# Interleaving the moving columns of three-product matmuls, and placing the weight panels 64 bytes apart

## What is computed

```python
def swiglu(h, w1, w3, w2):
    return (jax.nn.silu(h @ w1) * (h @ w3)) @ w2

def moe_swiglu(h, router_w, w1, w3, w2):
    ...
    for e in range(N_EXPERTS):
        out = out + gates[..., e:e + 1] * swiglu(h, w1[e], w3[e], w2[e])
    return out

def second_block(...):
    for i in range(DEPTH):
        ...
        h_x = h_x + 0.5 * mx[2] * ffn1(pre(h_x, g_norm[i, 0], mx[0], mx[1]))
        ...
        h_x = h_x + mx[5] * ox
        h_x = h_x + 0.5 * mx[8] * ffn2(pre(h_x, g_norm[i, 2], mx[6], mx[7]))
```

## Time and profile before

| | |
|---|---|
| median of two runs | 2837.01 us (2836.5 and 2837.52) |
| the profiled execution's own time | 2839.29 us |
| its span, first to last instruction | 2837.6 us |
| PE busy | 2720.8 us, 96% of the span |
| PEld busy | 2445.7 us, 86% |
| DVE busy | 1913.8 us, 67% |
| ACT busy | 1182.6 us, 42% |
| mean traffic from HBM | 179 GB/s |
| mean granted TensorE clock | 0.989 of full speed |

### The profile page before, as it was taken

How to read it: one execution, slowest core, us unless ns; L and a number is a source line. 1 busy time by engine, 2 the same in 40 slices (tenths; PEclk the granted TensorE clock), 3 DMA queues, 4 the chain that set the end, 5 groups by cost and what they waited for, 6 DMA issues and landing times.

```text
span 2837.6 us, 43022 instructions
## 1 busy us (share of the span) xinstructions
PE 2720.8 (96%) x17542; PEld 2445.7 (86%) x17542; DVE 1913.8 (67%) x2703; ACT 1182.6 (42%) x1510; POOL 118.1 (4%) x227
## 2 busy tenths in 40 slices
PE   3979999999999999899999999999999999999999
PEld 3879998899999999888888888888888888886999
DVE  5877778765777788777477445764666646675655
ACT  3436445453443477642132424422334222255543
POOL 0010000000000000000000000000000000000000
PEclk9989999999999999999999999999999999999999
DMA  7676766635676698745355223453534534311554
GB/s 296 220 244 228 263 228 213 232 135 169 235 239 209 230 347 309 259 145 187 132 184 169 83 93 103 153 170 122 166 136 137 169 122 159 120 60 46 176 186 144
DMA packets 116619, 511.97 MB, mean 180 GB/s; under 512 B 12608, under 2 KB 16064, under 8 KB 116304
## 3 DMA queue, kind: packets, MB, share of 16 engines
q1 hardware_dynamic: 81776, 381.92, 39.5%
q0 software_dynamic: 32112, 117.45, 12.5%
q10 hardware_dynamic: 2544, 9.96, 0.9%
HBM read 508.24 MB, written 1.05 MB: 179 GB/s over the span
## 4 chain that ended last, share of the span: by engine, by line
PE 78%; DVE 11%; ACT 4%; issue 3%; DMA 2%; ACTq 0%; DVEq 0%; POOLq 0%
PE PS L2099 22%; PE PS L2101 22%; PE PS L2100 22%; DVE wlo L1102 5%; ACT whi L575 2%; PE PS L2293 1%; DMA ada_first<-in_adastream 1%; PE PS L2290 1%; PE PS L2289 1%; DVE ada L1134 1%; PE PS L2194 1%; DMA ada<-in_adastream 1%; PE PS L2195 1%; PE PS L2198 1%; DVE PS L1134 1%
## 5 line engine op out<-in xcount | busy, mean ns | idle before, releaser
L575 ACT ACTIVATE whi<-raw 128x1408 fp32r<-128x1408 f32 (+2 forms) x540 | 718.1, 1342 | 778.9 <-PE PS L2101 719.3
L1102 DVE TENSOR_TENSOR wlo<-raw,whi 128x1408 fp32r<-128x1408 f32 (+2 forms) x540 | 839.8, 1577 | 217.0 <-ACT whi L575 216.1
L2099 PE MATMUL PS<-h_hi,whi 128*128 128x256 f32 (+1 forms) x2656 | 859.2, 324 | 15.5 <-DVE wlo L1102 8.4
L2100 PE MATMUL PS<-h_lo,whi 128*128 128x256 f32 (+1 forms) x2656 | 858.7, 323 | 0.0
L2101 PE MATMUL PS<-h_hi,wlo 128*128 128x256 f32 (+1 forms) x2656 | 858.6, 323 | 0.0
L2099 PEld LDWEIGHTS PS<-h_hi,whi 128*128 128x128 f32 x2656 | 499.6, 188 | 64.0 <-DVE wlo L1102 11.4
L2100 PEld LDWEIGHTS PS<-h_lo,whi 128*128 128x128 f32 x2656 | 499.6, 188 | 43.1 <-issue 0.2
L2101 PEld LDWEIGHTS PS<-h_hi,wlo 128*128 128x128 f32 x2656 | 500.1, 188 | 39.6
L2099 PE MATMUL PS<-hid_hi,whi 128*128 128x256 f32 (+1 forms) x1298 | 415.3, 320 | 4.3 <-DVE wlo L1102 4.3
L2100 PE MATMUL PS<-hid_lo,whi 128*128 128x256 f32 (+1 forms) x1298 | 414.6, 319 | 0.0
L2101 PE MATMUL PS<-hid_hi,wlo 128*128 128x256 f32 (+1 forms) x1298 | 414.4, 319 | 0.0
(11 more groups left out here) (464 smaller groups left out, 3245.8 us busy)
## 6 DMA issues: line engine op xcount, KB each, us to landing
raw<-in_wstream SPq DMA_DIRECT2D x243, 704.0 KB, 4.5
raw<-in_wstream SPq DMA_DIRECT2D x176, 768.0 KB, 5.6
ada<-in_adastream POOLq DMA_DIRECT2D x222, 512.0 KB, 4.5
raw<-in_wstream SPq DMA_DIRECT2D x121, 512.0 KB, 4.0
ada_first<-in_adastream ACTq DMA_DIRECT2D x6, 1536.0 KB, 22.9
X<-in_xT SPq DMA_DIRECT2D x1, 1024.0 KB, 13.9
X<-in_ctxT SPq DMA_DIRECT2D x1, 1024.0 KB, 5.6
cond<-in_c_rows POOLq DMA_DIRECT2D x1, 1024.0 KB, 5.7
```

The source lines that it names most:

```text
L575: nc.scalar.activation(whi[:, (q + dp) % SLOTS, 0:n], raw[:, (q + dp) % RAW_SLOTS, 0:n], ACT.Copy).then_inc(hi_split, 1)
L1102: nc.vector.tensor_tensor(wlo[:, (q + dp) % SLOTS, 0:n], raw[:, (q + dp) % RAW_SLOTS, 0:n], whi[:, (q + dp) % SLOTS, 0:n].bitcast(F32), AL ...
L2099: mm(o, left[0], right[0], start=start, stop=False)
L2100: mm(o, left[0], right[1], start=False, stop=False)
```

## The change

No instruction is added, removed or moved on any engine. Two things are different in them: the order in which columns are read and written, and addresses.

1. All matmuls of the nine lines whose moving operand has at least 256 columns read these columns, and write their outputs, in another order. `zipped` cuts the columns in two halves and each half in runs of 16 (64 bytes of float32). The order is: run 0 of the first half, run 0 of the second half, run 1 of the first half, run 1 of the second half, and so on. Input and output are cut in the same way, so each result lands in the same place as before. The halves lie 512 bytes apart where there are 256 columns, and 1024 where there are 512.
2. `whi` and `wlo` become four tensors each, laid down in pairs (`whi0`, `wlo0`, `whi1`, ...), with an unused tensor of 64 bytes between the pairs. A panel's place so starts 12,352 bytes after the one before: 64 bytes further on in a block of 512.
3. The small tables (`tables`, `mod1`, `amp1` and others) are laid down ahead of the panels and not behind `stage_b`; `wroute_lo` shares its room with `amp2`; `turned_hi`, `turned_lo` and `picks` stand ahead of `gt`, `gi`, `rt` and `order`. By the addresses that result, tiles of the panels now start at 448, 0, 64 or 128 bytes of a block of 512 for places 0 to 3, and `h_hi`, `h_lo`, `hid_hi`, `hid_lo`, `few_hi`, `few_lo`, `cq_hi`, `turned_hi` at 128.

```diff
+LINE = 16
...
+        tables = sb("tables", [PART, VECS + CONSTS])
...
+        rstd = sb("rstd", [PART, 32])
         raw = sb("raw", [PART, RAW_SLOTS, SLOT * PART])
-        whi = sb("whi", [PART, SLOTS, SLOT * PART], F32R)
-        wlo = sb("wlo", [PART, SLOTS, SLOT * PART], F32R)
+        whi, wlo = [], []
+        for i in range(SLOTS):
+            whi.append(sb(f"whi{i}", [PART, SLOT * PART], F32R))
+            wlo.append(sb(f"wlo{i}", [PART, SLOT * PART], F32R))
+            if i < SLOTS - 1:
+                sb(f"shift{i}", [PART, 16])
...
+            def zipped(x):
+
+                return x.rearrange("p (s j e) -> p j s e", s=2, e=LINE) if x.shape[-1] >= SEQ else x
+
             def passes(o, left, right, start, stop):
 
-                mm(o, left[0], right[0], start=start, stop=False)
-                mm(o, left[0], right[1], start=False, stop=False)
-                return mm(o, left[1], right[0], start=False, stop=stop)
+                o, high, low = zipped(o), zipped(right[0]), zipped(right[1])
+                mm(o, left[0], high, start=start, stop=False)
+                mm(o, left[0], low, start=False, stop=False)
+                return mm(o, left[1], high, start=False, stop=stop)
 
             def weights(q, tile):
                 w = slice(PART * tile, PART * tile + PART)
-                return whi[:, q % SLOTS, w], wlo[:, q % SLOTS, w]
+                return whi[q % SLOTS][:, w], wlo[q % SLOTS][:, w]
...
-                    mm(o, left[0], right[0], start=k == 0, stop=False)
-                    mm(o, left[1], right[0], start=False, stop=False)
+                    mm(zipped(o), left[0], zipped(right[0]), start=k == 0, stop=False)
+                    mm(zipped(o), left[1], zipped(right[0]), start=False, stop=False)
                 h_chunk(n, k, half)
                 for o, left, right in tiles:
-                    ins = mm(o, left[0], right[1], start=False, stop=k == KD - 1)
+                    ins = mm(zipped(o), left[0], zipped(right[1]), start=False, stop=k == KD - 1)
```

More of the change, by code:

```diff
@@ L194, in sem @@
             return ctx.enter_context(nc.semaphore(name))
-        raw = sb("raw", [PART, RAW_SLOTS, SLOT * PART])
-        whi = sb("whi", [PART, SLOTS, SLOT * PART], F32R)
-        wlo = sb("wlo", [PART, SLOTS, SLOT * PART], F32R)
+        tables = sb("tables", [PART, VECS + CONSTS])
+        vec, con = tables[:, 0:VECS], tables[:, VECS:VECS + CONSTS]
+        mod1 = sb("mod1", [PART, 2, 48])
+        with ExitStack() as s:
+            wga = sb("wga", [PART, 2, KD, RANK], F32, s)
+        mod2 = sb("mod2", [PART, 2, 72, 2])
+        amp1 = sb("amp1", [PART, 2, 2, KD])
+        with ExitStack() as s:
+            wroute_lo = sb("wroute_lo", [PART, KD, N_EXPERTS], F32R, s)
+        amp2 = sb("amp2", [PART, 2, 3, KD, 2])
+        with ExitStack() as s:
+            wroute = sb("wroute", [PART, KD, N_EXPERTS], F32, s)
+        gate2 = sb("gate2", [PART, 2, 3, KD, 2])
+        ms = sb("ms", [PART, 36])
+        root = sb("root", [PART, 32])
+        rstd = sb("rstd", [PART, 32])
+        raw = sb("raw", [PART, RAW_SLOTS, SLOT * PART])
+        whi, wlo = [], []
[4 more added lines that the diff above has]
+                sb(f"shift{i}", [PART, 16])
         with ExitStack() as s:
@@ L220, in build @@
         stage_b = sb("stage_b", [PART, 2, BOTH])
[L221 to L234, removed]
         h_hi, h_lo, hid_hi, hid_lo = {}, {}, {}, {}
@@ L264, in build @@
                 gated = sb("gated", [PART, 2, SEQ], F32, s2)
+                turned_hi = sb("turned_hi", [PART, 2, D], F32R, s2)
+                turned_lo = sb("turned_lo", [PART, 2, D], F32R, s2)
+                picks = sb("picks", [PART, 2, SPARSE, PART], F32R, s2)
                 gt = sb("gt", [PART, 2, 64], F32, s2)
@@ L288, in build @@
                 wroute_hi = sb("wroute_hi", [PART, KD, N_EXPERTS], F32R, s2)
-                wroute_lo = sb("wroute_lo", [PART, KD, N_EXPERTS], F32R, s2)
             with ExitStack() as s2:
@@ L574, in split_hi @@
                     act.wait_ge(panel_used, USED0 + q - SLOTS + 1 + dp)
-                nc.scalar.activation(whi[:, (q + dp) % SLOTS, 0:n], raw[:, (q + dp) % RAW_SLOTS, 0:n], ACT.Copy).then_inc(hi_split, 1)
+                nc.scalar.activation(whi[(q + dp) % SLOTS][:, 0:n], raw[:, (q + dp) % RAW_SLOTS, 0:n], ACT.Copy).then_inc(hi_split, 1)
             def square(T, g, group):
@@ L1101, in split_lo @@
                     dve.wait_ge(panel_used, USED0 + q - SLOTS + 1 + dp)
-                nc.vector.tensor_tensor(wlo[:, (q + dp) % SLOTS, 0:n], raw[:, (q + dp) % RAW_SLOTS, 0:n], whi[:, (q + dp) % SLOTS, 0:n].bitcast(F32),
+                nc.vector.tensor_tensor(wlo[(q + dp) % SLOTS][:, 0:n], raw[:, (q + dp) % RAW_SLOTS, 0:n], whi[(q + dp) % SLOTS][:, 0:n].bitcast(F32),
                                         ALU.subtract).then_inc(lo_split, 1)
@@ L2288, in ffn @@
                                 pe.wait_ge(evacuated, g0 - 1 + EXPERT_GROUPS * i)
-                            mm(bank, left[0], right[0], start=k == 0, stop=False)
-                            mm(bank, left[1], right[0], start=False, stop=False)
+                            mm(zipped(bank), left[0], zipped(right[0]), start=k == 0, stop=False)
+                            mm(zipped(bank), left[1], zipped(right[0]), start=False, stop=False)
                         h_chunk(norm_of_h, k, half)
                         for o, (bank, left, right) in enumerate(tiles):
-                            ins = mm(bank, left[0], right[1], start=False, stop=k == KD - 1)
+                            ins = mm(zipped(bank), left[0], zipped(right[1]), start=False, stop=k == KD - 1)
                             if places[o][1] == PANEL - 1:
@@ L2350, in values @@
                                 ins = passes(PS[:, 2 + t, :], (hi[:, k, tok], lo[:, k, tok]),
-                                             (whi[:, q % SLOTS, w], wlo[:, q % SLOTS, w]), k == 0, k == KD - 1)
+                                             (whi[q % SLOTS][:, w], wlo[q % SLOTS][:, w]), k == 0, k == KD - 1)
                         ins.then_inc(panel_used, 1)
@@ L2785, in tokens_out @@
                         w = slice(512 * b, 512 * b + 512)
-                        ins = passes(PS[:, bank + b, :], (ckv_hi[:, tok], ckv_lo[:, tok]), (whi[:, q, w], wlo[:, q, w]), True, True)
+                        ins = passes(PS[:, bank + b, :], (ckv_hi[:, tok], ckv_lo[:, tok]), (whi[q][:, w], wlo[q][:, w]), True, True)
                     return ins
```

3 lines of the change are left out of this document (removed).

## The result

The changed kernel takes 2911.39 us (median of 2910.36 and 2912.42) against 2837.01 us: slower by a ratio of 1.0261 with a 95% interval of 1.0236 to 1.0285. The forecast was 2783 us and the range 2690 to 2900 us, so both the sign and the range missed. The profiled execution took 2910.36 us, with a span of 2908.7 us, 71.1 us over that of before.

What follows compares the result with a forecast made beforehand. PE's matmul pace was taken to bound the kernel. Gains of 43 us (256 token columns) and 14 us (512) made 57, less 5% for waits 54: 2839.3 - 54 = 2785.3 us profiled, 2783 against the median; range 2690 to 2900 us.

Steps and rivals of the forecast that it cites:

- The 5% that I took off for waits: Whole kernel: 5% taken off the 57 us gain for waits that appear, leaving 54 us.
- the two parts that I had split it into: Ordered matmuls' surplus over streaming time: 4.7 ns per second block of 256 columns, 6.5 ns once per matmul.
- the price of the turned read: Matmuls with turned columns: 113.3 ns for 256 token columns, 226.6 for 512; together 57 us gained, nothing for moving panels.
- The argument behind that step: Moving read and weight load differ in speed, one overtaking the other per matmul; turned halves keep the moving read from overtaking.
- The slow rival: All turned matmuls: breaks and lockstep make the kernel slower, 2977 us or, weaker, 2850; chance 0.26, of which 0.18 over 2894.
- Its first form: Turned matmuls: each run of 16 opens a new address in SBUF and PSUM, giving 2977 us.
- the price of 0.41 ns per break: Each new break after a run of 16 costs 6.6 / 16 = 0.41 ns; as lower bound, 140 us lost.
- The clause: Argument for the slow rival: halves share an offset of 512 bytes, so successive runs ask for one place; no size given.
- The weaker form: Place 3: panel and activation both start at 128, slowest by 3 ns; on a quarter of matmuls 12 us, 2850 us.
- The signs to look for: Weight-load starts: forecast 113 to 114 and 226 to 227 ns; no effect 118 and 229; slower 120 and over 240.

Runs made afterwards that it cites:

- steps of five: Kernel before, outputs in order; moving read takes runs of 16 columns at 0, 5, 10 and 15 times 64 bytes, again and again: 2838.2 us, ratio 0.9998.

## Why the prediction was wrong

**What held.** PE's pace sets the time and nearly all of its change arrives: 87 us of longer matmuls became 71 us. (The 5% that I took off for waits were 14 of 87 us, 16%, and came from waits that shrank.) The other engines' work and the tables' new addresses cost nothing. The pace depends on where the moving and the loaded operand start: the runs with new places alone change it, with the same work on DVE, ACT and the transfers. And the turned read lost just this dependence: with it all distances give 120.0 and 240.0 ns. The surplus of the ordered read, too, has the two parts that I had split it into, in so far as the best distance for 512 columns leaves 226.8 ns, 17 cycles for 16 columns, and the worst puts 6 ns on top.

**The step that failed** is the price of the turned read: "Between them I take the pace that the trace has already with the other distance, 113.3 ns for 256, and twice that, 226.6 ns, for 512, because it is the nearest row: the same instruction, the same column count, only other places." It was the nearest row in instruction and count, but its read was ordered, and the order was the thing that changed. Nor was it twice that for 512 columns: the kernel before has matmuls of 512 columns at this same distance, 3, those with `y_hi` and `y_lo` moving, which start at 64 bytes with `whi` and `wlo` at 128; six of them take 1.40 us, 233 ns each, where I had 226.6:

```profile
1712.24 0.19 PEld L2099 LDWEIGHTS PS<-y_hi,whi 128*128 128x128 f32 x1
...
1713.64 0.19 PEld L2099 LDWEIGHTS PS<-y_hi,whi 128*128 128x128 f32 x1
```

The runs put 120.0 and 240.0 ns in its place, 2.4 ns more and not 4.6 less for the 256 token columns, and 11 more and not 2.7 less for 512: +87 us in the sum and not -57. The argument behind that step looked at one of two relations, the moving read against the load beside it. The other, each run of the moving read against the run before it, costs more: in the order of the change it brings the matmul to 18 cycles per 16 columns whatever the load does, 13 ns over the best ordered read of 512 columns, where all that could be won from the load was about 4 ns in 256 columns (119.8 to 115.6) and 6 in 512.

**The rivals.** The slow rival had the sign. Its first form, each break costing at SBUF or PSUM, gave 2977 us and was twice too dear; the price of 0.41 ns per break, one cycle in 16 columns, was nearly right for 512 columns (11 ns over 32 runs is 0.35 ns) and too high for 256 (2.4 ns over 16 runs is 0.15), since the turned read gives back what the load had cost. But a break as such costs nothing, as the runs with writes alone and with steps of five show. The clause "each half again lands on the same offset of 512 bytes as the other, so two successive runs ask for one and the same place" came nearest to what the runs show, with 256 in place of 512 and as one case of a dependence on the order; I had given it a sentence and not a price. The weaker form, panel and activation both at distance 0 costing 3 ns, was wrong for the changed kernel: with turned reads place 3 costs no more than the others. With ordered reads it holds for 256 columns (119.6 ns against 116.5), while for 512 distance 0 is the best there is. The signs to look for were right: 120 and over 240 ns in all stretches alike had been written down, and 120.0 and 240.0 were measured.

## What to carry to other kernels

Before columns are read in another order, write down for each run of 64 bytes which quarter of 256 bytes it lies in: on this chip, with float32r operands, an order that keeps 0, 1, 2, 3 was free with both kinds of jumps that were tried, and every other order cost something. Turning in runs of 64 bytes between halves whose distance is a multiple of 256 bytes gives 0, 0, 1, 1, which cost 2.6% of the kernel here. Writes to PSUM in runs of 16 float32 were free, so an order of columns in such runs is to be judged by its read alone, and where PE's pace is the bound, a pad ahead of an operand (128 to 320 bytes here, for 0.6 and 0.75%) is worth a run.

## What the hardware showed that was not expected

- An ordered float32r read of 512 columns takes 226.8 to 233.1 ns at full clock by the distance of moving and loaded start modulo 256 bytes; 256 columns take 114.5 to 119.8 ns, with another order of the distances (3 is best for 256 and worst for 512). With 256 columns the distance isn't all: at distance 3 the panels moving in the kernel before take 114.5 ns, and the tokens in the run with places alone 116.7. Why is not shown: the load beside the matmul was never taken away.
- Even the best is 17 cycles for 16 columns (226.7 ns would be exact). Reading one and the same 64 bytes doesn't remove the one, it adds to it (241.0 ns).
- Runs of 8 and 4 columns from either half in turn cost 243.3 and 250.6 ns: 0.23 and 0.17 ns per run over the ordered read, against 0.35 with runs of 16.
- Turned reads make the pace steady: of 4,740 matmuls with 512 columns of `h` or `hid` moving in the run with turns alone 4,738 lie exactly 240 ns before the next, where most of the ordered ones of the kernel before take 226, 229 or 232 ns.
